# A GEMM with its operands exchanged, gelu values turned on PE, and three queues rearranged around a scatter

## What is computed

```
def peer(h, w_q, sub_keys, expert_u, expert_v):
    q = (xt @ w_q).reshape(T, PEER_HEADS, 2, PEER_DQ // 2)
    s = jnp.einsum('thpd,hpnd->thpn', q, sub_keys)
    s_half, i_half = lax.top_k(s, PEER_TOPK)
    ...
    top_s, pos = lax.top_k(cand, PEER_TOPK)
    idx = jnp.take_along_axis(cand_idx, pos, axis=-1)
    g = jax.nn.softmax(top_s, axis=-1)
    ...
        a = jnp.einsum('cd,ced->ce', xc, expert_u[ic])
        w = (gc * jax.nn.gelu(a)).astype(xc.dtype)
        return jnp.einsum('ce,ced->cd', w, expert_v[ic])
```

## Time and profile before

| | us |
|---|---|
| median of 3 runs | 3717.65 |
| lowest, highest | 3714.27, 3719.58 |
| profiled execution, its time | 3711.69 |
| profiled execution, its span | 3709.9 |
| PE busy, of the span | 3319.0 (89%) |
| DVE / ACT / POOL busy | 2029.6 / 1471.7 / 547.1 |
| `peer_u`, first load issued | 509.4 |
| scatters, first and last issued | 749.73 and 1311.58 |

### The profile page before, as it was taken

How to read it: one execution, slowest core, us unless ns; L and a number is a source line. 1 busy time by engine, 2 the same in 40 slices (tenths; PEclk the granted TensorE clock), 3 DMA queues, 4 the chain that set the end, 5 groups by cost and what they waited for, 6 DMA issues and landing times.

```text
span 3709.9 us, 50142 instructions
## 1 busy us (share of the span) xinstructions
PE 3319.0 (89%) x21070; PEld 3024.1 (82%) x21070; DVE 2029.6 (55%) x2847; ACT 1471.7 (40%) x1851; POOL 547.1 (15%) x364
## 2 busy tenths in 40 slices
PE   5978999997353569999999999999999899999998
PEld 4767899997353569988888887898999799999996
DVE  5766548883121134566666666555446555555556
ACT  3335444443111134444444444444444454444443
POOL 2100000078888720000000000000000000000000
PEclk8989999998776789999999999999999999999999
DMA  8313555676454466676666655544455555555554
GB/s 321 119 46 101 164 190 190 203 199 149 69 103 67 105 215 207 211 248 243 238 238 234 237 190 176 182 154 162 148 181 181 193 168 190 188 188 187 187 189 153
DMA packets 214961, 659.43 MB, mean 178 GB/s; under 512 B 56096, under 2 KB 56096, under 8 KB 212176
## 3 DMA queue, kind: packets, MB, share of 16 engines
q1 hardware_dynamic: 160928, 581.96, 47.9%
q0 software_dynamic: 53808, 74.27, 8.3%
HBM read 620.35 MB, written 35.78 MB: 177 GB/s over the span
## 4 chain that ended last, share of the span: by engine, by line
PE 67%; POOL 12%; issue 3%; DVE 3%; ACT 1%; DMA 1%; DVEq 0%; ACTq 0%; POOLq 0%
PE bank L1284 67%; POOL scr_g L2205 12%; DVE wlo L1705 1%; DMA scr_g<-M 1%; PE bank L1326 1%; ACT whi L1474 1%; ACT M L1464 0%; DMA M<-scr_g 0%; POOL scr_a L2214 0%; DVE TMP L1768 0%; DVE R L2133 0%; DVE TMP L1769 0%; ACT M L1516 0%; DVE AL L1745 0%; DVE ST L1783 0%
## 5 line engine op out<-in xcount | busy, mean ns | idle before, releaser
L1705 DVE TENSOR_TENSOR wlo<-raw,whi 128x1024 fp32r<-128x1024 f32 x1101 | 1349.2, 1229 | 1375.5 <-ACT whi L1474 1371.9
L1474 ACT ACTIVATE whi<-raw 128x1024 fp32r<-128x1024 f32 x1101 | 1159.5, 1059 | 1404.8 <-PE bank L1284 1399.0
L1284 PE MATMUL bank<-AH,whi 128*128 128x256 f32 (+1 forms) x4112 | 1181.7, 287 | 253.2 <-DVE wlo L1705 252.8
L1284 PE MATMUL bank<-AL,whi 128*128 128x256 f32 (+1 forms) x4112 | 1171.4, 285 | 0.0
L1284 PE MATMUL bank<-AH,wlo 128*128 128x256 f32 (+1 forms) x4112 | 1171.2, 285 | 0.0
L1284 PEld LDWEIGHTS bank<-AH,whi 128*128 128x128 f32 (+1 forms) x4112 | 797.1, 194 | 258.3 <-DVE wlo L1705 255.2
L1284 PEld LDWEIGHTS bank<-AL,whi 128*128 128x128 f32 (+1 forms) x4112 | 797.2, 194 | 0.9
L1284 PEld LDWEIGHTS bank<-AH,wlo 128*128 128x128 f32 (+1 forms) x4112 | 796.4, 194 | 0.1
L1284 PE MATMUL bank<-whi,BH 128*128 128x512 f32 (+1 forms) x1608 | 625.7, 389 | 0.5 <-DVE wlo L1705 0.4
L1284 PE MATMUL bank<-wlo,BH 128*128 128x512 f32 (+1 forms) x1608 | 623.6, 388 | 0.0
L1284 PE MATMUL bank<-whi,BL 128*128 128x512 f32 (+1 forms) x1608 | 623.3, 388 | 0.0
(11 more groups left out here) (238 smaller groups left out, 1953.6 us busy)
## 6 DMA issues: line engine op xcount, KB each, us to landing
raw<-in_peer_u SPq DMA_DIRECT2D x256, 512.0 KB, 4.2
raw<-in_peer_v SPq DMA_DIRECT2D x256, 512.0 KB, 3.6
raw<-in_w_in SPq DMA_DIRECT2D x160, 512.0 KB, 3.3
raw<-in_w_up SPq DMA_DIRECT2D x128, 512.0 KB, 3.9
raw<-in_w_down SPq DMA_DIRECT2D x128, 512.0 KB, 3.4
raw<-in_w_out SPq DMA_DIRECT2D x64, 512.0 KB, 4.1
raw<-in_w_in_a SPq DMA_DIRECT2D x32, 512.0 KB, 5.7
scr_g<-M POOLq DMA_DIRECT2D x8, 2048.0 KB, 35.4
```

The costliest lines, as they stand in the source:

```text
L1284: return e.matmul(outp, l, r, start=start, stop=stop)
L1474: e.activation(whi[:, n % NH, :], raw[:, n % NR, :], ACT.Copy).then_inc(s_hi, 1)
L1705: e.tensor_tensor(wlo[:, n % NH, :], raw[:, n % NR, :], bf(whi[:, n % NH, :]), ALU.subtract).then_inc(s_lo, 1)
```

## The change

1. `peer_u` is cut with `cut` in place of `cut_t` and multiplied by `gemm`: 128 tokens stationary, 512 weight columns moving, 12 matmuls a piece. The result has tokens on partitions. Gelu goes into new buffers `gtok`; a task `later()` has PE turn the 8 blocks of 128 x 128 (4 in each of two banks), ACT copies the first bank into `gels`, DVE the second.
2. `gelu_store` moves from POOL's queue to SP's, among the loads of the pieces.
3. `gate_blank` and the 8 `gate_clear` DMAs move from the start to behind the attention stage, ahead of the second load of x.
4. `routing()` finishes token half 0 before it begins the top 16 of half 1. One task `scatter()` issues for both halves, 4 scatters per step and not 2 per half, rounds of the two halves in turn where both have rounds left.

```
-                    if k % 2:
+                    if k % 4 == 3:
                         yield
...
             def routing():
+                tasks.append(scatter())
                 for t in range(2):
                     for hp in range(16):
                         go("top16", SC[:, t, hp, :], V16[:, t, hp, :], I16u[:, t, hp, :], fresh("DVE", t_sc, everything))
                         last = up("DVE", "top16")
                         yield
-                go("i16_cast", fresh("DVE", last))
-                last = up("DVE", "i16_cast")
-                for t in range(2):
+                    go("i16_cast", t, fresh("DVE", last))
+                    last = up("DVE", "i16_cast")
...
-                    tasks.append(scatter(t, [tg, up("DVE", "expert_ids")]))
+                    routed.append([tg, up("DVE", "expert_ids")])
...
+                def later():
+                    yield
+                    yield
+                    gi, gfree = yield from wait_for(gel_slots)
+                    ends = []
+                    for m in range(2):
+                        bank, bfree = yield from wait_for(misc)
+                        tk = transposed([gtok[ti][:, t, 128 * k:128 * k + 128] for k in (2 * m, 2 * m + 1) for t in range(2)],
+                                        bank, tg, bfree)
+                        yield
+                        if m == 0:
+                            go("gelu_turned_a", gi, bank, fresh("ACT", tk, gfree))
+                            ends.append(up("ACT", "gelu_turned_a"))
+                        else:
+                            go("gelu_turned_v", gi, bank, fresh("DVE", tk, gfree))
+                            ends.append(up("DVE", "gelu_turned_v"))
+                        misc.give(bank, ends[-1])
+                    tok_slots.give(ti, tk)
+                    yield
+                    go("gelu_store", j, gi, fresh("SP", ends))
...
-                pair, b, last = gemm_t("peer_u", 8 * j, 16, AH, AL, nA)
+                pair, b, last = gemm("peer_u", 8 * j, 16, AH, AL, nA)
```

More of the change, by code:

```diff
@@ L791, in walk @@
             om_free = everyone()
+            go("gate_blank")
+            t_blank = up("POOL", "gate_blank")
+            for c in range(8):
+                go("gate_clear", c, fresh("POOL", t_blank))
+                t_clear = landing("gate_cleared")
             pml = Slots(ps3 + [M[:, 512 * i:512 * i + 512] for i in range(3)], om_free)
@@ L877, in walk, with scatter @@
             g_written = []
[L879 to L883, removed]
+            routed = []
+            def scatter():
+                landed, rounds, t = [t_clear, t_clear], [0, 0], 1
+                while len(g_written) < 2:
+                    while not routed:
+                        yield
+                    if len(routed) == 2 and rounds[1 - t] < 8:
+                        t = 1 - t
+                    elif len(routed) == 1:
+                        t = 0
+                        if rounds[0] == 8:
+                            yield
+                            continue
+                    h = rounds[t]
+                    for k in range(16):
+                        go("gate_scatter", t, 16 * h + k, fresh("POOL", routed[t], landed[t] if k == 0 else None))
                         mark = landing(f"gate_scattered{t}")
-                        if k % 2:
+                        if k % 4 == 3:
                             yield
-                    landed = mark
-                g_written.append(landed)
+                    landed[t] = mark
+                    rounds[t] += 1
+                    if rounds[t] == 8:
+                        g_written.append(mark)
             def routing():
+                tasks.append(scatter())
                 for t in range(2):
@@ L1588, in gate_exp, with gelu, gelu_turned @@
                 act(idg[2], idg[2], ACT.Exp, "gate_exp")
-            def gelu(gi, b, ready):
+            def gelu(ti, b, ready):
                 for mark in ready:
                     e.wait_ge(*mark)
[L1593 to L1596, removed]
+                e.activation(gtok[ti][:, 0, :], b[0][:, :], ACT.Gelu_apprx_tanh)
+                act(gtok[ti][:, 1, :], b[1][:, :], ACT.Gelu_apprx_tanh, "gelu")
+            def gelu_turned(gi, bank, ready):
+                for mark in ready:
+                    e.wait_ge(*mark)
+                act(gels[gi][:, 0:2, :], banks[bank][:, :].rearrange("p (k n) -> p k n", k=2), ACT.Copy, "gelu_turned_a")
             def expert_split(sc, k0, ready, _):
@@ L2024, in expert_ids, with gelu_turned @@
                 e.tensor_copy(EID[t], idg[0]).then_inc(sem("expert_ids"), 1)
+            def gelu_turned(gi, bank, ready):
+                for mark in ready:
+                    e.wait_ge(*mark)
+                e.tensor_copy(gels[gi][:, 2:4, :], banks[bank][:, :].rearrange("p (k n) -> p k n", k=2)
+                              ).then_inc(sem("gelu_turned_v"), 1)
             def expert_gate(sc, k0, ready):
```

45 lines of the change are left out of this document (22 added, 23 removed).

## The result

| | before | after |
|---|---|---|
| median, us | 3716.55 (4 runs) | 3736.80 (4 runs) |
| lowest, highest | 3714.27, 3719.58 | 3733.21, 3737.78 |
| profiled execution, time | 3711.69 | 3733.21 |
| ratio to before, with its 95% interval | | 1.0052 [1.0035, 1.0070] |

The forecast was 3741, in a range from 3710 to 3800; the measured 3736.8 lies 4 us under it. The profiled execution was forecast at 3735 and took 3733.21. The sum is right to 2 us. Its terms are less good, and part of that is luck: two of them missed in opposite directions. The most useful thing in this case came out of one that was wrong: the scatters were not as long as I had them, for a reason that the experiments then turned into a gain of its own.

What follows compares the result with a forecast made beforehand. The prediction took DVE's wait for the fetch after the last scatter as the limit: landing -66, pieces behind it +106.5, part 1 -0.5, start -16.6, together +23.4, giving 3741 us from a median of 3717.65; range 3710 to 3800.

Steps and rivals of the forecast that it cites:

- The gate sets the end: DVE's wait for the fetch after the last scatter: stage ends at that landing, plus restart, plus pieces behind the wait.
- PE's idle stretch: Before the last scatter lands, PE was to be full until some 930, then idle about 300 us.
- The pieces behind the gate: `peer_u` pieces after DVE's wait for the last scatter: 113, not 76, adding 106.5 us, less 0.5 for part 1.
- The landing: Last scatter's landing: 66 us earlier on the old clock, with 16.6 more from the start; expected near 1231.
- The start: Clears moved away from the kernel's start: gain 16.6 us, bounds 8 to 19; constants first used near 10.5.
- the first scatter: Start of the scatters on POOL: at 692 on the old clock, not 749.73; near 675 with the start gain.
- The rounds beside busy engines: Rounds of 16 scatters while other engines run: 40.7 us each, bounds 37.4 to 44.3; 6.2 rounds done by 945.
- those beside idle engines: Rounds of 16 scatters while PE is idle: 31.1 us each, bounds 31.1 to 34.6.
- Part 1 at half a microsecond: Exchanged `peer_u` GEMM with turning: 2.876 us a piece against 2.88, so 113 pieces gain 0.5 us.
- the first rival: Scatters undisturbed: what lengthens them belongs to the old kernel alone, all 16 rounds take 31.1 us; 3681 us, chance 0.13.
- collision: Rival at the clears' new place: they hold up `w_out` weights and x, start gain lost, 3758 us; chance 0.12.
- Stores: Gelu stores moved to SP: ACT's 239.1 us of waiting goes, but lies ahead of the gate; priced at 0.

Runs made afterwards that it cites:

- b_sp: The kernel before with only the gelu stores moved from POOL's queue to SP's: 3709.37 us, ratio 0.9979.
- b_order: The kernel before with only half 0 routed first and one task issuing 4 scatters a step: 3761.04 us, ratio 1.0118.
- a_late: The changed kernel with fetch(0), fetch(1) and prepare(0) moved behind the last piece of `peer_u`: 3478.23 us, ratio 0.9365 to the kernel before.
- b_late: The kernel before with fetch(0), fetch(1) and prepare(0) moved behind the last piece of `peer_u`: 3694.05 us, ratio 0.9941.
- b_clears: The kernel before with only the blank and eight clears moved behind the attention stage: 3700.23 us against 3717.58, ratio 0.9957.
- b_gemm: The kernel before with only the `peer_u` GEMM exchanged and gelu values turned, stores still on POOL: 3675.10 us, ratio 0.9885.
- a_dve: The changed kernel with only 32 of 1024 low-part columns subtracted on DVE for `peer_u` pieces: 3703.07 us (one run).
- a_noorder: The changed kernel with routing and scatters in the order of before: 3663.58 us, ratio 0.9863 to the kernel before.
- a_late_noorder: The changed kernel with before's routing and scatter order, and fetch(0), fetch(1), prepare(0) behind the last `peer_u` piece: 3493.63 us, ratio 0.9405 to before.
- a_mix: a_late with 4 rounds, not 8, issued while only half 0 is routed, so rounds of the halves alternate: 3459.59 us, ratio 0.9314 to before.

## Why the prediction was right, step by step

**The gate sets the end: right.** What bounds the kernel was read from the earlier trace rows, and b_sp, b_order, a_late and b_late show it from four sides. PE's idle stretch took 308.2 us where about 300 were forecast, and 321 us of `peer_u` stand behind it (1247 to 1568), where 325 were.

**The pieces behind the gate: +101.2 where +106.5 - 0.5 stood.** The number of pieces, 113, is exact. A block takes 22.72 us and not 23.01. The block of `w_in_2` was near, but in it one of the two groups of transposes takes longer. From the same chain of the kernel before:

```profile
2297.86 0.66 PE bank L1326 x4
...
2301.27 0.44 PE bank L1326 x4
```

In the changed kernel both take 0.44 us. That is 0.22 of the 0.29 us. From that row I took 0.5 us for part 1 behind the gate, where 0.32 us a block, some 4.5 us in 14 blocks, were to be had.

**The landing: -80.35 where -82.6 stood, by terms that cancel, which is luck.** The start gave 12.6 us at the first load of `peer_u`, not 16.6 (alone it gave 15.7). The constants were used at 11.98 and not 10.5; part of that is my sum, since 441 KB at the pace of the x load are 1.8 us and not 1.3. At `w_kv_b` 14.0 us were left (its first load at 148.18 in place of 162.21). With the start taken off, the first scatter came 55.7 us earlier and not 57.7. So it stood at 681.47 and not 675. The rounds beside busy engines, mis-sized the other way, took 38.0 us ((947.52 - 681.47) / 7), where the term was 40.7; those beside idle engines 31.9 ((1234.30 - 947.52) / 9), where it was 31.1.

**Part 1 at half a microsecond: wrong, and this step failed in its reasoning.** I priced the GEMM by its pieces behind the gate and kept for the scatters the pace of the old kernel. That PE's form sets DVE's cadence, and DVE's cadence whether scatters are held, was left out, though the earlier trace rows show a held and a free scatter: 42 us alone. I had the first rival ask just this (what lengthens scatters might belong to the old kernel alone) and gave it 0.13; it happened in part, 38.0 on the way from 40.7 to 31.1. (By its own terms its mean round would decide at 33.4 us, not at the 33.7 that I wrote; that changes nothing here.)

**Parts taken alone do not add up.** Alone: -17.4, -8.2, +43.5, -42.5, in all -24.6; together +20.3. Of the missing 45, 16 are between the first three parts and 30 are part 4's: in this company the landing moves 35 us with it (1269.66 to 1234.30) and not 58. Once the others have shortened the stage, the order pays for half 0 ahead of half 1 with eight more landing waits (12.6 to 30.5 us) and with the other gaps (3.0 to 14.2). The forecast was right in sum because it priced the parts as a whole kernel, from one first scatter to one gate.

**Clears: right.** No collision; by the medians b_clears gained 17.4 where 16.6 stood. **Stores: right**, 0 forecast and 8 measured alone, nothing in company.

## What to carry to other kernels

When a wait for a slow chain stands in the queue of an engine that others need, ask first how much work is queued behind it: moving that wait was worth 259 us here (23 us where the stores behind the scatters took over as the limit), and moving the chain forward by 80 us together with the wait was a loss. Price a rearrangement as a whole, from its first event to its last, since parts that share a stage do not add. When one engine's instructions hold up another's and their periods agree (2.58 + 0.30 against 2.88 us), the hold repeats itself; cutting the holding instruction in two shortened the hold and broke the repetition here.

## What the runs showed of the hardware that I had not expected

A running two-input subtraction of DVE holds an indirect DMA of POOL only at its beginning, to the end of the one instruction, even with another right behind it: 1.97 us behind a half of some 0.65, up to 2.58 behind one of 1.23, 1.55 where the scatter starts first. A scatter that starts within 0.04 us of the subtraction goes free and the subtraction takes 1.27 to 1.30 us instead (one in the kernel before, eight in b_gemm), so the earlier one is not always the one that holds.

In the kernels a_late, a_dve and after, gaps of 1.8 to 4.9 us stand behind the same six scatters (numbers 60, 113, 120, 188, 241 and 248), 12 to 17 us over the usual gap. With the stores on POOL's queue there are none. With the stores on SP but the scatters in before's order one is left (behind number 113 in b_sp and a_noorder, behind 60 in a_late_noorder), in a_mix two (behind 60 and 252). No run here tells why; it stays open.
